# Attention rebuilt in pairs of heads on two row halves of the array, with two weight buffers and a pair's transposes one step behind its scores

## What is computed

```python
# layers 0 and 1: window attention, a query block of 128 sees its own and the previous key block
s = einsum('qhgd,khd->hgqk', q, k) * D ** -0.5            # 8 heads, 2 key/value heads, D = 64
p = softmax(concatenate([where(valid, s, -1e30), sink]))[..., :-1]
a_out = einsum('hgqk,khd->qhgd', p, v) * silu(ag)          # gated
# "even" layer: window attention with sinks over 768 tokens, and a latent attention (8 heads of 96)
# "odd" layer: plain attention, and a differential one that joins two softmaxes of the same values
o = softmax(q1 @ k1.T) @ v - lam * softmax(q2 @ k2.T) @ v  # 4 such heads, values 128 wide
```

## Time and profile before

| what | us |
|---|---|
| median of 3 runs | 2904.19 |
| lowest, highest | 2891.95, 2906.38 |
| span of the profiled execution | 2906.3 |
| PE, DVE, ACT, POOL busy | 2460.7, 1459.9, 841.4, 934.2 |
| attention: layer 0, layer 1 | 42.5, 42.7 |
| attention: even, latent first, latent second, odd | 105.8, 67.9, 67.9, 197.5 |

### The profile page before, as it was taken

The page is one execution under the profiler, slowest core; times in us unless marked ns, Lnnn a source line. Parts: engine busy times, 40 slices in busy tenths (PEclk is TensorE's granted clock), DMA queues, the critical chain, the costliest instruction groups (busy, mean ns, idle before and its releaser), DMA issues. The chain is left out here.

```text
span 2906.3 us, 32667 instructions
## 1 busy us (share of the span) xinstructions
PE 2460.7 (85%) x12562; PEld 2053.4 (71%) x12562; DVE 1459.9 (50%) x2490; ACT 841.4 (29%) x1544; POOL 934.2 (32%) x572
## 2 busy tenths in 40 slices
PE   2888667988675988999689999999598997799997
PEld 2777355777354866668479998989487776588886
DVE  4776644876635956447752342222588665300112
ACT  2215113215113155443232121211412443322222
POOL 1431225320235210001354242433652001555554
PEclk9999768988777999899789999999799999899999
DMA  6540012530021310002322232332260000133222
GB/s 227 169 147 8 0 59 90 163 110 1 0 87 48 122 52 1 1 1 79 114 66 95 84 105 80 102 91 69 78 194 29 1 1 22 59 101 95 94 94 73
DMA packets 141906, 218.97 MB, mean 75 GB/s; under 512 B 12148, under 2 KB 64916, under 8 KB 141624
## 3 DMA queue, kind: packets, MB, share of 16 engines
q1 hardware_dynamic: 141752, 216.88, 23.4%
HBM read 214.75 MB, written 2.10 MB: 75 GB/s over the span
## 5 line engine op out<-in xcount | busy, mean ns | idle before, releaser
L284 POOL TENSOR_TENSOR w_lo<-w_raw,w_hi 128x1024 fp32r<-128x1024 f32 (+3 forms) x252 | 591.3, 2347 | 1306.0 <-ACT w_hi L277 1306.0
L277 ACT ACTIVATE w_hi<-w_raw 128x1024 fp32r<-128x1024 f32 (+3 forms) x252 | 255.4, 1017 | 1222.1 <-PE ps L297 986.6
L295 PE MATMUL ps<-w_hi,h_transposed 128*128 128x512 f32 (+3 forms) x1088 | 416.8, 383 | 44.2 <-DVE proj_one L678 20.8
L296 PE MATMUL ps<-w_lo,h_transposed 128*128 128x512 f32 (+3 forms) x1088 | 408.4, 375 | 0.0
L297 PE MATMUL ps<-w_hi,h_transposed 128*128 128x512 f32 (+3 forms) x1088 | 408.0, 375 | 0.0
L295 PE MATMUL ps<-h_transposed,w_hi 128*128 128x384 f32 (+1 forms) x1056 | 373.7, 354 | 3.6 <-issue 2.1
L296 PE MATMUL ps<-h_transposed,w_hi 128*128 128x384 f32 (+1 forms) x1056 | 373.2, 353 | 0.0
L297 PE MATMUL ps<-h_transposed,w_lo 128*128 128x384 f32 (+1 forms) x1056 | 373.1, 353 | 0.0
L355 DVE SCALAR_TENSOR_TENSOR mod_acc_aux<-w_raw,c_act,mod_acc_aux 128x512 f32<-128x512 f32 x280 | 275.4, 1008 | 46.4 <-DMA w_raw<-in_w_mod_dram 24.9
L295 PEld LDWEIGHTS ps<-w_hi,h_transposed 128*128 128x128 f32 x1088 | 212.7, 195 | 85.9 <-POOL w_lo L284 24.1
L1141 DVE TENSOR_TENSOR ffn_full<-ps,ffn_silu 128x768 f32<-128x768 f32 (+1 forms) x44 | 34.2, 819 | 423.6 <-PE ps L297 423.6
(11 more groups left out here) (297 smaller groups left out, 3847.8 us busy)
## 6 DMA issues: line engine op xcount, KB each, us to landing
w_raw<-in_ada_w_dram SPq DMA_DIRECT2D x96, 512.0 KB, 4.2
w_raw<-in_ffn_w_in_dram SPq DMA_DIRECT2D x88, 512.0 KB, 3.6
w_raw<-in_w_mod_dram SPq DMA_DIRECT2D x48, 512.0 KB, 4.6
w_raw<-in_ffn_w_out_dram SPq DMA_DIRECT2D x44, 512.0 KB, 3.6
w_raw<-in_w_in_dram SPq DMA_DIRECT2D x40, 512.0 KB, 4.6
w_raw<-in_w_out_dram SPq DMA_DIRECT2D x16, 512.0 KB, 4.4
w_raw<-in_od_w_in_dram SPq DMA_DIRECT2D x16, 512.0 KB, 4.6
mod_gain<-in_norm_g_dram SPq DMA_DIRECT2D x16, 256.0 KB, 4.1
```

The lines of the kernel that those rows point to most:

```text
L277: act.activation(w_hi[:, i % 2, 0:k * n], w_raw[:, u % 4, 0:k * n], ACT.Copy).then_inc(w_hi_ready.sem, 1)
L284: pool.tensor_tensor(w_lo[:, i % 2, 0:k * n], w_raw[:, u % 4, 0:k * n], w_hi[:, i % 2, 0:k * n].bitcast(F32), ALU.subtract).then_inc(w_lo_ ...
L295: pe.matmul(acc, left[0], right[0], start=start, stop=False)
L296: pe.matmul(acc, left[0], right[1], start=False, stop=False)
```

## The change

`Attention` now takes steps. A step is a pair of heads of one query block. What it does:

- **Scores.** Head 0 of the pair is read from partitions 0 to 63, head 1 from 64 to 127, so a pair's scores are two products on the two row halves of the array. Keys need no zeroed copy. (The latent heads keep 96 rows.) The factor 1/8 goes into the copies that make the queries.
- **Probabilities are divided before they are transposed.** DVE makes the inverse sums of a pair (`inverse`), and POOL multiplies both halves of the row by them (L990). With sinks, POOL also adds the sink to the bias (L982), ahead of that in its loop.
- **Sums features first.** The value product has the values (64 columns) as stationary and the transposed probabilities as moving operand, the two heads on two column halves of one bank. The output comes out with features on partitions, already transposed, so `MixTransposed` no longer transposes it (`ready`). The gate AG is transposed in `Pieces` instead, 16 more transposes in each of layers 0 and 1.
- **Joined heads** keep the probabilities as stationary operand, and one inverse at the end.
- **Buffers.** There are two probability buffers, `lag` is 1. In a pass of the loop PE issues the scores of step s, the first round (up to four transposes) of step s - 1, the sums of step s - 2, then the other rounds of step s - 1. A round is copied from the one bank 7 (the third from bank 6).

```diff
+            TURN_BANK, SUM_BANK = 7, 6
...
+                self.slots = 3 if self.wide else 6
+                self.lag = len(probs) - 1
...
+                for s, rounds in enumerate(self.rounds):
+                    if not self.wide:
+                        by = [s % 2]
+                    elif self.has_join[s]:
+                        by = [0, 0]
+                    else:
+                        by = [[0], [0, 1], [0, 0, 1]][len(rounds) - 1]
+                    self.kept.append([(sem, sem.plan(1) + 1) for sem in ((s_kept_a, s_kept_v)[v] for v in by[:len(rounds)])])
...
+            def score(self, pe, s):
+                x, w = self.steps[s], self.width(s)
+                for i in range(2):
+                    self.wait(pe, s_exp, 2 * s + i - self.slots + 1)
+                runs = range(len(x["keys"][0]))
+                for k in runs:
+                    c, m = x["keys"][0][k][1], x["keys"][0][k][0].shape[-1]
+                    masks = [(z, mc) for z, mc in x["masks"] if c <= mc < c + m]
+                    done = []
+                    for i in range(2):
+                        sc = self.scores(2 * s + i, w)
+                        done.append(pe.matmul(sc[:, c:c + m], x["q"][i], x["keys"][i][k][0], start=True, stop=not masks))
+                    for i in range(2):
+                        sc = self.scores(2 * s + i, w)
+                        for z, mc in masks:
+                            done[i] = pe.matmul(sc[:, mc:mc + P], identb[:, :], z, start=False, stop=(mc == masks[-1][1]))
+                    if k == runs[-1]:
+                        for ins in done:
+                            ins.then_inc(s_scored.sem, 1)
...
+                for b, v in enumerate(x["values"]):
+                    if self.has_join[s]:
+                        ins = pe.matmul(ps[:, self.SUM_BANK, 0:P], probs_t[:, b * P:(b + 1) * P], v, start=(b == 0), stop=(b == nb - 1))
+                    else:
+                        for i in range(2):
+                            ins = pe.matmul(ps[64 * i:64 * i + 64, self.SUM_BANK, 0:P], v[i], probs_t[:, (i * nb + b) * P:(i * nb + b + 1) * P],
+                                            start=(b == 0), stop=(b == nb - 1))
...
             def tensor(self, pe):
-                n = len(self.units)
+                n = len(self.steps)
+                for loop in range(n + self.lag + 1):
+                    t, v = loop - self.lag, loop - self.lag - 1
+                    if loop < n:
+                        self.score(pe, loop)
+                    if 0 <= t < n:
+                        self.turn(pe, t, 0)
+                    if 0 <= v < n:
+                        self.sum(pe, v)
+                    if 0 <= t < n:
+                        for r in range(1, len(self.rounds[t])):
+                            self.turn(pe, t, r)
...
             def scalar(self, act):
+                for loop in range(n + self.lag):
+                    t, s = loop - self.lag, loop
+                    if 0 <= t < n:
+                        self.keep(act, s_kept_a, t, 0)
+                    if s < n:
+                        self.exponent(act, s, 0)
+                    if 0 <= t < n:
+                        for r in range(1, len(self.rounds[t])):
+                            self.keep(act, s_kept_a, t, r)
+                    if s < n:
+                        self.exponent(act, s, 1)
+                        if self.steps[s]["sink"] is not None:
+                            r = 2 * s % 16
+                            self.wait(act, s_arg, s + 1)
+                            act.activation(self.st[:, 3, r:r + 2], self.st[:, 1, r:r + 2], ACT.Exp).then_inc(s_sunk.sem, 1)
...
+            def inverse(self, dve, s):
+                st, r = self.st, 2 * s % 16
+                self.wait(dve, s_exp, 2 * s + 2)
+                total = st[:, 2, r:r + 2]
+                if self.steps[s]["sink"] is not None:
+                    self.wait(dve, s_sunk, s + 1)
+                    dve_s.chain(dve.tensor_tensor(st[:, 4, r:r + 2], total, st[:, 3, r:r + 2], ALU.add))
+                    total = st[:, 4, r:r + 2]
+                ins = dve.reciprocal(st[:, 5, r:r + 2], total)
+                ins.then_inc(s_inv.sem, 1)
+                if self.has_join[s]:
+                    w, probs = self.width(s), self.probs[s % len(self.probs)]
+                    self.wait(dve, s_inv, s + 1)
+                    dve_s.chain(dve.scalar_tensor_tensor(out=st[:, 6, r:r + 1], in0=st[:, 5, r + 1:r + 2], scalar=self.neg_lambda,
+                                                         in1=st[:, 2, r:r + 1], op0=ALU.mult, op1=ALU.mult))
+                    dve.scalar_tensor_tensor(out=probs[:, w:2 * w], in0=probs[:, w:2 * w], scalar=st[:, 6, r:r + 1], in1=probs[:, 0:w],
+                                             op0=ALU.mult, op1=ALU.add).then_inc(s_joined.sem, 1)
...
             def vector(self, dve):
+                for loop in range(n + self.lag + 1):
+                    s, t, v = loop, loop - self.lag, loop - self.lag - 1
+                    if self.lag == 1 and 1 <= s <= n:
+                        self.inverse(dve, s - 1)
+                    if s < n:
+                        for heads in ([[0], [1]] if self.wide else [[0, 1]]):
+                            self.maximum(dve, s, heads)
+                    if 0 <= v < n:
+                        self.finish(dve, v)
+                    if self.lag == 2 and 1 <= s <= n:
+                        self.inverse(dve, s - 1)
+                    if 0 <= t < n:
+                        for r in range(len(self.rounds[t])):
+                            self.keep(dve, s_kept_v, t, r)
...
             def gpsimd(self, pool):
+                n, st = len(self.steps), self.st
+                for loop in range(n + 1):
+                    if loop < n and self.steps[loop]["sink"] is not None:
+                        r, h = 2 * loop % 16, self.steps[loop]["sink"]
+                        self.wait(pool, s_max, 2 * loop + 2)
+                        pool.tensor_tensor(st[:, 1, r:r + 2], st[:, 0, r:r + 2], self.sinks[:, h:h + 2], ALU.add).then_inc(s_arg.sem, 1)
+                    s = loop - 1
+                    if s >= 0 and not self.has_join[s]:
+                        w, probs = self.width(s), self.probs[s % len(self.probs)]
+                        self.wait(pool, s_inv, s + 1)
+                        for i in range(2):
+                            r = (2 * s + i) % 16
+                            p = probs[:, i * w:(i + 1) * w]
+                            pool.tensor_scalar(p, p, st[:, 5, r:r + 1], None, ALU.mult).then_inc(s_norm.sem, 1)
...
-        probs2, probs2_t = take("att_probs_two", [P, 2, TOK]), take("att_probs_t_two", [P, 2, TOK])
+        qaT, kaT = take("even_q_t", [P, 4, TOK]), take("even_k_t", [P, 2, TOK])
+        probs2 = [take(f"att_probs_two{i}", [P, 2 * TOK]) for i in range(2)]
+        probs2_t = [take(f"att_probs_t_two{i}", [P, 2 * TOK]) for i in range(2)]
...
+                schedule.append(Attention(steps, probsb, probsb_t, stats))
+            schedule.append(MixTransposed(None, XT + CT, [PE_[:, :, kt * P:(kt + 1) * P] for kt in range(KT)]))
...
+            groups += [dict(ops=tiles_of(AG + pair * P, P), dsts=[(0, P, P1[:, 0:XT, AG + pair * P:AG + (pair + 1) * P])]) for pair in range(4)]
```

More of the change, by code:

```diff
@@ new lines, in __init__ @@
+                self.b[s_norm], self.b[s_joined] = s_norm.plan(2 * plain), s_joined.plan(joined)
+                self.order = [sum(j == k for k in self.has_join[:s]) for s, j in enumerate(self.has_join)]
+                turned = [nb if j else 2 * nb for nb, j in zip(self.blocks, self.has_join)]
+                self.rounds = [[(i, min(4, m - i)) for i in range(0, m, 4)] for m in turned]
+                self.turn0 = [sum(len(r) for r in self.rounds[:s]) for s in range(n + 1)]
+                self.b[s_turned] = s_turned.plan(self.turn0[n])
@@ new lines, in turn @@
+            def turn(self, pe, s, r):
+                first, count = self.rounds[s][r]
+                if self.has_join[s]:
+                    self.wait(pe, s_joined, self.order[s] + 1)
+                    at0 = self.width(s)
+                else:
+                    self.wait(pe, s_norm, 2 * self.order[s] + (first + count - 1) // self.blocks[s] + 1)
+                    at0 = 0
+                if self.bank_free[s, r]:
+                    sem, n = self.bank_free[s, r]
+                    pe.wait_ge(sem.sem, n)
+                for i in range(count):
+                    c = at0 + (first + i) * P
+                    ins = pe.transpose(ps[:, self.turn_bank(r), i * P:(i + 1) * P], self.probs[s % len(self.probs)][:, c:c + P], ident)
+                ins.then_inc(s_turned.sem, 1)
@@ new lines, in maximum @@
+            def maximum(self, dve, s, heads):
+                u, w, m = 2 * s + heads[0], self.width(s), len(heads)
+                r = u % 16
+                self.wait(dve, s_scored, u + m)
+                if m == 2:
```

(12 more changed lines are left out.)

413 lines of the change are left out of this document (181 added, 232 removed).

## The result

The changed kernel takes 3217.2 us (median of 4 runs, 3215.1 to 3220.8), the kernel before 2901.2 in the same comparison: ratio 1.109, 95% interval 1.107 to 1.112. The forecast was 3011, range 2960 to 3070. The direction held; the rise is 316 us where 107 were forecast.

What follows compares the result with a forecast made beforehand. PE's list bounds the attention phases before the change, an unhidden loop between pairs mostly after it; 86 + 53 - 5 - 25 - 2 = +107 us on the profiled 2906.3 gives 3013, stated as 3011 us, range 2960 to 3070.

Steps and rivals of the forecast that it cites:

- The loop from one pair's first exp to the next pair's: Attention phases: with two buffers nothing hides this chain; 5.65 us a pair by these loops against 4.7 before.
- POOL's place behind the maxima: Phases with sinks: POOL's sink addition precedes the previous pair's multiplication, putting the next maxima (0.87 us at two blocks) in the loop.
- the halves overlap: PE array: products on two halves run together; a six-block pair costs 3.9 us (latent 5.15) against 6.6 before.
- the rival of hidden loops: Attention phases: loops are hidden and the busiest engine bounds each phase; 2742 us, chance 0.10.
- the one of halves that don't overlap: PE sums: halves run one after another at 0.43 us a block; 3070 us, chance 0.05.
- The copy between two exps: Wide phases, ACT: the previous pair's second-round copy delays the second exp; at five blocks it starts at 1.05, not 0.79.
- POOL's price: POOL's multiplication L990: 0.43, 0.66, 0.78, 0.90 us at 256, 512, 640, 768 columns.
- nearer to the memset: POOL's multiplication: one operand read, one written, so costed near the memset's 0.92 ns a column, the lower bound.
- the other bound: POOL's multiplication, upper bound from two-input operations: 0.77, 1.35, 1.64, 1.93 us at 256, 512, 640, 768 columns.
- Rival three: POOL's multiplication runs at its two-input rate: +67 us, 3078 us, chance 0.10.
- Half clock: PE at the 1.2 GHz level: 1.6 us more per two pairs in layers 0 and 1; 4 for even's last eight.
- around it: Around the attention: `Pieces` +1.5 us each in layers 0 and 1, `MixTransposed` about -1 four times; together -2.

Runs made afterwards that it cites:

- multiply_first: The changed kernel with POOL's two multiplications of a pair ahead of the next pair's sink addition, nothing else: 3089.0 us.
- exps_together: The changed kernel with both exps of a pair (and the sink exp) on ACT ahead of the previous pair's second- and third-round copies: 3179.9 us.
- busy_pe: The changed kernel with unread 256-column products on PE before each wait for multiplied weights, five in layer 0, ten in layer 1: 3197.5 us.
- busy_pe_wide: The changed kernel with unread PE products before each pair's first transposes, ten in even, five in first latent stretch and odd: 3196.2 us.
- three_and_dve: The changed kernel with a third probability buffer (not in the first latent stretch) and the multiplications on DVE: 2887.0 us, ratio 0.993 to the kernel before.
- three_dve_tuned: three_and_dve with all layer 0 attention copies on ACT and POOL's second low part after the first four subtractions: 2868.7 us, ratio 0.988.
- best_three: The changed kernel with DVE multiplications, third buffer except latent, ACT copies in layers 0 and 1, both exps first, later POOL low part: 2869.8 us, ratio 0.988.

## Why the forecast was right in kind and wrong in size

**What held.** The loop from one pair's first exp to the next pair's, through inverse, multiplication, transposes and copy, sets the pace; POOL's place behind the maxima is in it (multiply_first); the halves overlap; the rival of hidden loops and the one of halves that don't overlap fell. The copy between two exps is a term (exps_together).

**The step that failed first: POOL's price.** The forecast took 0.43 to 0.90 us, "nearer to the memset", because the operation reads one operand. Measured, it is 0.92 to 2.20, past the other bound. Put into the forecast's own loops:

- layers 0 and 1: 2 x 0.495 on the 12 pairs of two blocks, and 2 x 0.3 on the four of one block (0.60 measured, 0.31 by the forecast's rate): 14 us each;
- even: 1.105, 0.905 and 2 x 0.495 on 8 pairs each, as a pair of two blocks needs both multiplications for its one round: 24 us;
- latent: 5.3 + 1.3 = 6.6 instead of PE's 5.7 on 8 pairs and 2 x 0.495 on 4: 11 us each (6.91 measured between first exps, 1466.70 to 1473.61; the second copy starts 1.70 after the exp, where 1.3 was forecast);
- odd: 16 x 1.3, 21 us.

Together that is 96 of the 200 us by which the forecast for the profiled span (3013) was short. Rival three had the mechanism, and priced it at 67.

```profile
1466.70 0.90 ACT L891 ACTIVATE att_probs_lat<-ps,attention_stats 128x768 f32<-128x768 f32 x1
...
1468.40 0.60 ACT L881 ACTIVATE att_probs_t_lat<-ps 128x512 f32<-128x512 f32 x1 [0.71 <-PE ps L840]
...
1473.61 0.90 ACT L891 ACTIVATE att_probs_lat<-ps,attention_stats 128x768 f32<-128x768 f32 x1
```

**The second: the clock, priced too low in layers 0 and 1 and hardly at all elsewhere.** Half clock was counted in layers 0 and 1 (9 us each) and for the even layer's last eight pairs (4). But PE waits 3.1 us per pair in layer 0 and 4.2 in the even layer, and its granted clock fell in all six stretches. In layer 0 the sum closes to 2 or 3 us: 76 forecast at full clock + 14 for POOL's price = 90, and busy_pe measured 87.8 at a clock of 0.98; the clock costs the other 17, not 9. In a pair of five blocks, 7.4 + 1.1 + 1.83 = 10.33 against 10.25 measured, and of the 1.83 busy_pe_wide took 1.55 away. So the slow multiplication is paid in the loop, and beside it PE idles and loses its clock. Moving it to DVE gave back 285 us. Of these 128 are the order, which multiply_first gives by itself; the 157 of the engine are more than the 96 of the bare price. That the rest of them is the clock's, which rose with it (0.58 to 0.80 in layer 0, 0.68 to 0.83 in the even layer), fits but was not measured apart.

**The third: around it.** Forecast -2, measured +17. Two-input subtractions from SBUF were costed like those from PSUM. Two of four waited behind POOL's subtractions of 1024 columns. The Trainium skill (SBUF — State Buffer, SBUF: two separate sides) says that a DVE operation with two SBUF inputs and a GpSimd operation that reads SBUF exclude each other for a whole instruction; the trace agrees (2.83 us in three_and_dve, beside a POOL record of 2.80, where 0.68 is usual), and the forecast should have used it. three_dve_tuned took 2.1 us of it away in one phase; the rest was not taken apart.

What stays open is the remaining excess in the latent layer (10 and 9 us a stretch), in the odd layer (21) and of 10 of the even layer's 33, of which busy_pe_wide took 23: the clock (0.68 in the even layer, 0.84 to 0.88 in the others) and the second-round copies act together. exps_together took 28.5 us from the odd layer, but its granted clock rose from 0.88 to 0.96 with it, and the added products were too dear there to separate the two.

**What it would take.** The rebuilt attention is worth having with its multiplication on DVE and a third buffer: 0.7% under the kernel before, and 1.2% with the edits of three_dve_tuned or best_three. In best_three that comes from the odd layer (145 against 197) and the even one (98 against 105); layers 0 and 1 stay 3 us above. Around the attentions 16 us more than before are left in best_three's profile, and 3 in three_dve_tuned's, so how much is left there is not settled.

## What to carry to other kernels

When every item of a loop lies on its critical path, an engine that is busy for a third of the time (POOL, 29 of 105 us in layer 0, 73.5 of 216 in the even layer) can set the pace: look at what ends the waits, not at the shares. An operation whose price is bracketed 1.8 to 2.1 times apart, and that stands twice in such a loop, deserves the upper bound in the sum, and its engine a second look; here even the upper bound was too low. And once PE is predicted to wait for microseconds in each round, price its items at the lower clock level as well, since that lengthens the same loop once more: 17 of layer 0's 105 us.

## What the hardware showed that I had not expected

POOL multiplies by a per-partition scalar at 2.5 ns a column, slower than it combines two tensors (2.3); DVE does the same in 0.35 us at 256 columns and 0.62 at 768. Useless products made a stretch faster: five of them per pair, 70.6 us of PE work instead of 54.0, took layer 0 from 104.8 to 87.8 us. A DVE subtraction of 512 columns can take 2.83 us instead of 0.68 when POOL subtracts beside it from SBUF.
